# A decoder trunk with experts on one core: the last strip's transposes and the fetched rows' transposes go between the two down pieces of the fifth strip

## The chip, the core and the metric

The kernel runs on one NeuronCore of a Trainium2 chip. TensorE (PE in the profile, its weight loads PEld) multiplies into the PSUM banks; ScalarE (ACT) and VectorE (DVE) work on elements; GpSimd (POOL) and SyncE (SP) here mostly issue transfers. Each engine runs its own queue of instructions in order; queues wait for each other by semaphores. The metric is the device time of one execution, in microseconds.

## What is computed

Two layers of a hybrid decoder over 256 tokens of width 1024, in float32. The second layer's feed-forward part is a mixture of 8 experts, each token going to 2 of them. This is the part that the change touches:

```python
def swiglu(h, w_gate, w_up, w_down):
    return (jax.nn.silu(h @ w_gate) * (h @ w_up)) @ w_down

def moe_ffn(h, w_router, w_gate, w_up, w_down):
    ...
    out = jnp.zeros_like(hf)
    for e in range(N_EXPERTS):
        out = out + gates[:, e:e + 1].astype(hf.dtype) * swiglu(hf, w_gate[e], w_up[e], w_down[e])
```

`w_gate[e]` and `w_up[e]` are 1024 x 2816, `w_down[e]` is 2816 x 1024.

## The kernel before

**Precision.** Each float32 operand is split into a high part (a rounded copy, float32r) and a low part (the rest), and every product is three matmuls: high times high, high times low, low times high (`mm3`, lines 1476 to 1480). Of a weight piece ScalarE makes the high part (`split_expert`, line 696, into `hi_ring`) and VectorE subtracts it from the raw piece (line 1010, into `lo_ring`). Both rings have three slots. The split of piece n + 3 may begin when TensorE has used piece n (`piece_used`), and TensorE begins piece n when `lo_ready` says so.

**Items and pieces.** The loop goes over items: an expert and up to 128 of its tokens, whose rows are gathered. With these inputs 8 items run, one for each expert. An expert's weights come in 33 pieces of 1 MB, in the order of `E_ORDER`. The 2816 hidden columns are cut into six strips (c = 0 to 5), five of 512 and the last of 256. A strip has gate pieces G, up pieces U and down pieces D, two of each (the last strip: one of each). The down pieces of strip c - 1 come behind the gate and up pieces of strip c. So an item ends with G5, U5, D4.0, D4.1, D5 (places 28 to 32 of the order, D4.0 being part 0 of the fifth strip's down pieces), and the next one begins with G0.0, G0.1, U0.0, U0.1. In iteration j of an item, ScalarE and VectorE first split piece j + 2, and then do what else belongs to piece j; the splits of pieces 33 to 35, so counted, belong to the next item.

**From gate and up to down.** With 128 tokens as the output's partitions, gate goes to bank 0 and up to bank 1. ScalarE applies silu (`m_sg`), VectorE multiplies (`m_prod`, line 1431). Then TensorE transposes the product, 128 columns at a time (`transpose_act`, line 1789, into bank 2 or 3), ScalarE copies the high part out (`m_hi`, line 979) and VectorE the low part (`m_lo`, line 1436), and the down pieces multiply these into banks 4 and 5. In general the transposes of strip c are issued behind the gate pieces of strip c + 1. The last strip has none behind it; its transposes stand in front of D5.

**The next item's rows.** GpSimd fetches the next item's rows by an indirect transfer (line 653) once VectorE has written their numbers (line 1454, at U4.0). TensorE transposes them, eight blocks (`fetched_transposes`, line 1774) into banks 6 and 7; ScalarE copies out `sel_hi` (line 953), VectorE `sel_lo` (line 1457). Both are views of hT_hi and hT_lo, and so they are called in the trace; the fetched rows and `m_prod` are views of `xn`. G0.0 waits for `sel_lo`.

**The item's result.** Behind D5 ScalarE copies banks 4 and 5 out as `y_hi` (line 984) and VectorE as `y_lo` (line 1461); the next item scatters them back to token order behind U0.0 and G1.0 (lines 1785 and 1786).

**Order of the queues around the change.** TensorE: D4.0, D4.1, two transposes of strip 5, eight of the fetched rows, D5. ScalarE: split 32, split 33, `m_hi`, split 34, two `sel_hi`, two `y_hi`, split 35. VectorE: split 32, split 33, `m_lo`, split 34, two `sel_lo`, two `y_lo`, split 35. This order is written out by hand. For the last item a branch skips splits 33 to 35.

Of the kernel before, what the change touches and what calls it, by code (L numbers as in the profile page):

```python
# [22 lines left out]
ALU = mybir.AluOpType  # L23
ACT = mybir.ActivationFunctionType
AX = mybir.AxisListType
F32 = mybir.dt.float32
# [5 lines left out]
D = 1024  # L32
# [94 lines left out]
EC = (FF + EW - 1) // EW  # L127
# [74 lines left out]
def build(nc, a, out):  # L202
    with ExitStack() as ctx:
# [8 lines left out]
        bank = [ctx.enter_context(nc.psum_tensor(f"bank{i}", [P, 512], F32)) for i in range(8)]  # L212
# [207 lines left out]
        gathered = sem("gathered")  # L420
# [15 lines left out]
        gathered_lo = sem("gathered_lo")  # L436
# [39 lines left out]
        def last_part(kind, c, part):  # L476
            return part == expert_width(c) // FC - 1
# [7 lines left out]
        def transposed_after(kind, c, part):  # L485

            if kind == "G" and c >= 1 and last_part(kind, c, part):
                return c - 1
            if kind == "D" and c == EC - 2 and last_part(kind, c, part):
                return EC - 1  # L490
            return None

# [188 lines left out]
        def _(act):  # L681
# [268 lines left out]
            def fetched_evac(i):  # L950
                for h in range(2):
                    act.wait_ge(gather_mm, 4 + 2 * i + h + 1)
                    A(sel_hi[:, 4 * h:4 * h + 4, :], bank[6 + h][:].rearrange("p (k s) -> p k s", k=4),
                      ACT.Copy).then_inc(gathered, 1)

            def item(i, more):

                for j, (kind, c, part) in enumerate(E_ORDER):
                    if j + 2 < NFF or more is True:
                        split_expert(i, j + 2)  # L960
                    else:
                        with act.If(more):
                            split_expert(i, j + 2)
                    w = expert_width(c)
                    if kind == "G" and last_part(kind, c, part):
                        act.wait_ge(piece_used, expert_done(i, "G", c))
                        act.wait_ge(prod_done, GU0 + c + i * EC)
                        A(m_sg[:, 0:w], bank[0][:, 0:w], ACT.Silu).then_inc(sg_done, 1)
                    if kind == "U" and c == 2 and part == 0:
                        act.wait_ge(onehot_tmm, i + 1)  # L970
                        A(onehot_t[:], bank[6][:, 0:TT * P].rearrange("p (t s) -> p t s", t=TT),
                          ACT.Copy).then_inc(onehot_tdone, 1)
                    tc = transposed_after(kind, c, part)
                    if tc is not None:
                        act.wait_ge(act_t, tc + 1 + i * EC)
                        if tc >= 2:
                            act.wait_ge(piece_used, expert_done(i, "D", tc - 2))
                        nf = expert_width(tc) // P
                        A(m_hi[:, tc % 2, 0:nf, :], bank[2 + tc % 2][:, 0:nf * P].rearrange("p (f s) -> p f s", f=nf),
                          ACT.Copy).then_inc(act_hi, 1)  # L980
                fetched_evac(i)
                act.wait_ge(piece_used, expert_done(i, "D", EC - 1))
                for h in range(2):
                    A(y_hi[:, h * 512:(h + 1) * 512], bank[4 + h][:], ACT.Copy).then_inc(yhi_done, 1)
# [14 lines left out]
        def _(dve):  # L999
# [418 lines left out]
            def item(i, more, first=False):  # L1418

                for j, (kind, c, part) in enumerate(E_ORDER):  # L1420
                    if j + 2 < NFF or more is True:
                        split_expert(i, j + 2)
                    else:
                        with dve.If(more):
                            split_expert(i, j + 2)
                    w = expert_width(c)
                    if kind == "U" and last_part(kind, c, part):
                        dve.wait_ge(sg_done, GU0 + c + 1 + i * EC)
                        dve.wait_ge(piece_used, expert_done(i, "U", c))
                        dve.wait_ge(act_t, c + i * EC)  # L1430
                        V.tensor_tensor(m_prod[:, 0:w], bank[1][:, 0:w], m_sg[:, 0:w], ALU.mult).then_inc(prod_done, 1)
                    tc = transposed_after(kind, c, part)
                    if tc is not None:
                        nf = expert_width(tc) // P
                        dve.wait_ge(act_hi, GU0 + tc + 1 + i * EC)
                        V.tensor_tensor(m_lo[:, tc % 2, 0:nf, :],  # L1436
                                        bank[2 + tc % 2][:, 0:nf * P].rearrange("p (f s) -> p f s", f=nf),
                                        m_hi[:, tc % 2, 0:nf, :].bitcast(F32), ALU.subtract).then_inc(act_lo, 1)
                    if not first and c <= 1 and kind == ("U", "G")[c] and part == 0:

                        scatter_add(i, 2 * c)
                        scatter_add(i, 2 * c + 1)
                    if kind == "D" and c == 2 and part == 0:

                        dve.wait_ge(onehot_tmm, i + 1)
                        dve.wait_ge(x_upd, XU0 + 4 * i)
                        V.tensor_copy(g_col[:], g_item[:, :, bass.ds(i, 1)].rearrange("p t o -> p (t o)")
                                      ).then_inc(route_v, 1)
                        dve.wait_ge(onehot_done, 3 + 3 * i)
                        make_onehot(i + 1)  # L1450
                        dve.wait_ge(route_v, rv[0] + 1 + i)
                    if kind == "U" and c == 4 and part == 0:
                        dve.wait_ge(slot_mm, i + 1)
                        V.tensor_copy(slot_i[:], bank[7][:, 0:1]).then_inc(slot_ready, 1)  # L1454
                for h in range(2):
                    dve.wait_ge(gathered, 4 + 2 * i + h + 1)
                    V.tensor_tensor(sel_lo[:, 4 * h:4 * h + 4, :], bank[6 + h][:].rearrange("p (k s) -> p k s", k=4),  # L1457
                                    sel_hi[:, 4 * h:4 * h + 4, :].bitcast(F32), ALU.subtract).then_inc(gathered_lo, 1)
                for h in range(2):
                    dve.wait_ge(yhi_done, 2 * i + 1 + h)  # L1460
                    V.tensor_tensor(y_lo[:, h * 512:(h + 1) * 512], bank[4 + h][:],
                                    y_hi[:, h * 512:(h + 1) * 512].bitcast(F32), ALU.subtract).then_inc(ylo_done[h], 1)
# [10 lines left out]
        def _(pe):  # L1473
# [322 lines left out]
            def item(i, first=False):  # L1796
                for j, (kind, c, part) in enumerate(E_ORDER):
# [1 line left out]
                    w = expert_width(c)  # L1799
                    wh, wl = expert_view(hi_of(NA + j), kind, c), expert_view(lo_of(NA + j), kind, c)  # L1800
                    if kind == "D":
                        if c == EC - 1:

                            transpose_act(i, c)
                            pe.wait_ge(onehot_tdone, i + 1)
                            fetched_transposes(i)
                        pe.wait_ge(act_lo, GU0 + c + 1 + i * EC)
                        for f in range(2):
                            for n in range(2):
                                ff = 2 * part + f  # L1810
                                r = mm3(bank[4 + n][:], m_hi[:, c % 2, ff, :], m_lo[:, c % 2, ff, :],
                                        wh[:, f, n * 512:(n + 1) * 512], wl[:, f, n * 512:(n + 1) * 512],
                                        c == 0 and ff == 0, c == EC - 1 and f == 1)
                    else:
                        if part == 0 and c >= 1:
                            if kind == "G":
                                pe.wait_ge(sg_done, GU0 + c + i * EC)
                            else:
                                pe.wait_ge(prod_done, GU0 + c + i * EC)
                        o = bank[0 if kind == "G" else 1][:, 0:w]  # L1820
                        for kk in range(PIECE // w):
                            k = part * (PIECE // w) + kk
                            if kind == "G" and c == 0 and k % 4 == 0:
                                if first:
                                    pe.wait_ge(gathered, 3 + k // 4)
                                else:
                                    pe.wait_ge(gathered_lo, k // 4 - 1 + 2 * i)
                            r = mm3(o, sel_hi[:, k, :], sel_lo[:, k, :], wh[:, kk, :], wl[:, kk, :],
                                    k == 0, k == KT - 1)
# [42 lines left out]
```

## Time and profile before

| | us |
|---|---|
| runs before | 1315.90, 1316.73, 1316.75 |
| median | 1316.73 |
| the profiled execution | 1313.38 |
| its span, from first to last instruction | 1311.6 |
| mean granted clock of TensorE | 0.976 |
| TensorE busy | 1243.0 (95%) |
| VectorE busy | 1021.0 (78%) |
| ScalarE busy | 822.2 (63%) |
| moved by DMA | 349.64 MB, mean 267 GB/s |

The trunk and the first layer fill the first 520 us or so. The rest is the loop over the items, and a short end: adding up and the last norm. Times in the timelines are microseconds from the span's start. A name such as `hT_lo<-bank,hT_hi` says what is written and from what. Matmuls overlap, so the distance from start to start is their true pace, and not their duration.

### The profile page before, as it was taken

How to read it: one execution, taken by the hardware profiler on the slowest of the kernel's cores; microseconds unless marked ns; L12 is line 12 of the kernel's file. 1: busy time of each engine (PE TensorE's matmuls, PEld its weight loads, DVE VectorE, ACT ScalarE, POOL GpSimd, SP SyncE). 2: the span in 40 equal slices, each digit the busy share in tenths (PEclk: the TensorE clock that was granted, in tenths of full speed). 3: DMA queues.
4: the chain of work that ended last, by engine and by line, in shares of the span. 5: the costliest groups of instructions: out<-in, count | busy, mean ns of one | idle time of the engine just before them, and what ended most of it. 6: DMA issues, size and time to landing. Idle time of an engine off the chain costs nothing.

```text
span 1311.6 us, 18352 instructions
## 1 busy us (share of the span) xinstructions
PE 1243.0 (95%) x6658; PEld 1051.2 (80%) x6658; DVE 1021.0 (78%) x1107; ACT 822.2 (63%) x862; POOL 144.9 (11%) x139
## 2 busy tenths in 40 slices
PE   6897999999899888999999999999999999999997
PEld 6866799999787676888888888888888888888885
DVE  5985655445678747888888888988988988988986
ACT  5366544443544745777777777777777776777774
POOL 2860000000068001000000000000000000000000
PEclk9989899999999797999999999999999999999998
DMA  9400665655452039999999999999999999999961
GB/s 332 156 10 1 226 198 192 191 179 181 125 165 76 6 105 393 379 361 354 351 363 355 350 362 355 350 361 355 349 363 356 350 359 361 347 360 362 342 236 48
DMA packets 176165, 349.64 MB, mean 267 GB/s; under 512 B 5719, under 2 KB 63637, under 8 KB 176116
## 3 DMA queue, kind: packets, MB, share of 16 engines
q1 hardware_dynamic: 173852, 341.27, 73.3%
q0 software_dynamic: 2064, 7.17, 1.5%
q8 instruction: 31, 0.51, 0.2%
q10 hardware_dynamic: 200, 0.54, 0.1%
q14 instruction: 18, 0.15, 0.0%
HBM read 346.87 MB, written 2.10 MB: 266 GB/s over the span
## 4 chain that ended last, share of the span: by engine, by line
PE 84%; DVE 8%; ACT 4%; issue 3%; DMA 0%; SPq 0%; POOL 0%; DVEq 0%; ACTq 0%; POOLq 0%
PE bank L1478 26%; PE bank L1480 25%; PE bank L1479 25%; PE bank L1793 1%; DVE cv L1126 1%; ACT hi_ring L696 1%; DVE lo_ring L1005 1%; PE bank L1575 1%; DVE xn L1126 1%; PE bank L1785 1%; ACT hi_ring L690 1%; PE bank L1786 1%; PE bank L1759 1%; PE bank L1615 1%; ACT e_sb L758 1%
## 5 line engine op out<-in xcount | busy, mean ns | idle before, releaser
L1010 DVE TENSOR_TENSOR lo_ring<-raw_m,hi_ring 128x2048 fp32r<-128x2048 f32 x168 | 383.0, 2288 | 54.9 <-ACT hi_ring L696 54.8
L696 ACT ACTIVATE hi_ring<-raw_m 128x2048 fp32r<-128x2048 f32 x168 | 323.0, 1923 | 83.0 <-PE bank L1480 83.0
L1478 PE MATMUL bank<-hi_ring,hT_hi 128*128 128x512 f32 (+2 forms) x896 | 337.7, 377 | 3.4 <-DVE hT_lo L1457 3.4
L1480 PE MATMUL bank<-hi_ring,hT_lo 128*128 128x512 f32 (+2 forms) x896 | 329.7, 368 | 0.0
L1479 PE MATMUL bank<-lo_ring,hT_hi 128*128 128x512 f32 (+2 forms) x896 | 329.4, 368 | 0.0
L1010 DVE TENSOR_TENSOR lo_ring<-raw_a,hi_ring 128x2048 fp32r<-128x2048 f32 x96 | 219.9, 2291 | 41.5 <-ACT hi_ring L696 41.4
L696 ACT ACTIVATE hi_ring<-raw_a 128x2048 fp32r<-128x2048 f32 x96 | 184.2, 1919 | 62.3 <-PE bank L1480 62.3
L1005 DVE TENSOR_TENSOR lo_ring<-raw_a,hi_ring 128x2048 fp32r<-128x2048 f32 (+2 forms) x59 | 132.2, 2246 | 93.9 <-ACT hi_ring L690 93.9
L1478 PEld LDWEIGHTS bank<-hi_ring,hT_hi 128*128 128x128 f32 x896 | 169.9, 190 | 34.8 <-DVE hT_lo L1457 6.4
L1480 PEld LDWEIGHTS bank<-hi_ring,hT_lo 128*128 128x128 f32 x896 | 169.7, 189 | 29.1
L1479 PEld LDWEIGHTS bank<-lo_ring,hT_hi 128*128 128x128 f32 x896 | 170.0, 190 | 27.1 <-issue 0.5
L1478 PE MATMUL bank<-hT_hi,hi_ring 128*128 128x256 f32 (+1 forms) x576 | 165.6, 288 | 1.5 <-DVE hT_lo L1040 1.5
L1479 PE MATMUL bank<-hT_lo,hi_ring 128*128 128x256 f32 (+1 forms) x576 | 164.3, 285 | 0.0
L1480 PE MATMUL bank<-hT_hi,lo_ring 128*128 128x256 f32 (+1 forms) x576 | 164.2, 285 | 0.0
L690 ACT ACTIVATE hi_ring<-raw_a 128x2048 fp32r<-128x2048 f32 (+2 forms) x59 | 109.9, 1862 | 69.1 <-PE bank L1480 62.6
L1478 PE MATMUL bank<-hi_ring,m_hi 128*128 128x512 f32 x352 | 140.2, 398 | 5.5 <-DVE m_lo L1436 5.5
L1479 PE MATMUL bank<-lo_ring,m_hi 128*128 128x512 f32 x352 | 139.4, 396 | 0.0
L1480 PE MATMUL bank<-hi_ring,m_lo 128*128 128x512 f32 x352 | 139.4, 396 | 0.0
L1478 PEld LDWEIGHTS bank<-hT_hi,hi_ring 128*128 128x128 f32 (+1 forms) x576 | 111.5, 194 | 2.7 <-issue 2.1
L1479 PEld LDWEIGHTS bank<-hT_lo,hi_ring 128*128 128x128 f32 (+1 forms) x576 | 111.6, 194 | 0.5
L1480 PEld LDWEIGHTS bank<-hT_hi,lo_ring 128*128 128x128 f32 (+1 forms) x576 | 111.4, 193 | 0.0
L652 POOL TENSOR_TENSOR pool_pad<-half_neg 128x1 f32<-128x1 f32 x8 | 17.3, 2157 | 753.7 <-DVE slot_i L1454 753.7
(277 smaller groups left out, 1399.4 us busy)
## 6 DMA issues: line engine op xcount, KB each, us to landing
raw_m<-in_w_down_exp SPq DMA_DIRECT2D x80, 1024.0 KB, 5.2
raw_a<-in_w_up_exp SPq DMA_DIRECT2D x48, 1024.0 KB, 5.3
raw_m<-in_w_gate_exp SPq DMA_DIRECT2D x48, 1024.0 KB, 5.5
raw_a<-in_w_gate_exp SPq DMA_DIRECT2D x40, 1024.0 KB, 5.5
raw_m<-in_w_up_exp SPq DMA_DIRECT2D x40, 1024.0 KB, 5.9
raw_a<-in_w_in SPq DMA_DIRECT2D x12, 1024.0 KB, 6.6
raw_a<-in_w_gate_dense SPq DMA_DIRECT2D x11, 1024.0 KB, 5.3
raw_a<-in_w_up_dense SPq DMA_DIRECT2D x11, 1024.0 KB, 5.5
```

Of the source, the lines that this page charges most:

```text
L652: nc.gpsimd.tensor_tensor(pool_pad[:], half_neg[:], half_neg[:], ALU.mult).then_inc(pad_done, 1)
L690: A(hi_of(n)[:, 0:w], t[:, 0:w], ACT.Copy).then_inc(hi_ready, 1)
L696: A(hi_of(NA + j), t, ACT.Copy).then_inc(hi_ready, 1)
L758: A(e[:, P:3 * P], s_sb[:, u % 3, P:3 * P], ACT.Exp, scale=-1.0, bias=neg_max[:, u, 1:2], accum_out=row_sum[:, u, 1:2]).then_inc(exp_done, 1)
L1005: V.tensor_tensor(lo_of(n)[:, 0:w], raw_slot(n)[0][:, 0:w], hi_of(n)[:, 0:w].bitcast(F32), ALU.subtract).then_inc(lo_ready, 1)
L1010: V.tensor_tensor(lo_of(NA + j), expert_slot(i, j)[0], hi_of(NA + j).bitcast(F32), ALU.subtract).then_inc(lo_ready, 1)
L1126: conv(V.scalar_tensor_tensor(out, win, wc, old, ALU.mult, ALU.add))
L1478: M(o, lh, rh, start=start, stop=False)
L1479: M(o, lh, rl, start=False, stop=False)
L1480: return M(o, ll, rh, start=False, stop=stop)
L1575: r = M(bank[1 + r3][0:QD, hh * T:(hh + 1) * T], w_uq[:, c, h * QD:(h + 1) * QD], cq[:, c, :], start=c == 0, stop=c == 1)
L1615: r = nc.tensor.transpose(bank[T_BANK[k % 2]][:, b * P:(b + 1) * P], e_sb[:, k % 3, 0, b * P:(b + 1) * P], ident)
```

## The change

TensorE does the transposes of the last strip and of the fetched rows between D4.0 and D4.1, and no longer between D4.1 and D5. ScalarE copies `m_hi` and both `sel_hi` out, and VectorE makes `m_lo` and both `sel_lo`, in the iteration of D4.0: behind split 32 and in front of split 33. Number and size of all instructions stay as they were.

```diff
--- before.py
+++ after.py
@@ -486,7 +486,7 @@
 
             if kind == "G" and c >= 1 and last_part(kind, c, part):
                 return c - 1
-            if kind == "D" and c == EC - 2 and last_part(kind, c, part):
+            if kind == "D" and c == EC - 2 and part == 0:
                 return EC - 1
             return None
 
@@ -978,7 +978,8 @@
                         nf = expert_width(tc) // P
                         A(m_hi[:, tc % 2, 0:nf, :], bank[2 + tc % 2][:, 0:nf * P].rearrange("p (f s) -> p f s", f=nf),
                           ACT.Copy).then_inc(act_hi, 1)
-                fetched_evac(i)
+                    if tc == EC - 1:
+                        fetched_evac(i)
                 act.wait_ge(piece_used, expert_done(i, "D", EC - 1))
                 for h in range(2):
                     A(y_hi[:, h * 512:(h + 1) * 512], bank[4 + h][:], ACT.Copy).then_inc(yhi_done, 1)
@@ -1436,6 +1437,13 @@
                         V.tensor_tensor(m_lo[:, tc % 2, 0:nf, :],
                                         bank[2 + tc % 2][:, 0:nf * P].rearrange("p (f s) -> p f s", f=nf),
                                         m_hi[:, tc % 2, 0:nf, :].bitcast(F32), ALU.subtract).then_inc(act_lo, 1)
+                    if tc == EC - 1:
+                        for h in range(2):
+                            dve.wait_ge(gathered, 4 + 2 * i + h + 1)
+                            V.tensor_tensor(sel_lo[:, 4 * h:4 * h + 4, :],
+                                            bank[6 + h][:].rearrange("p (k s) -> p k s", k=4),
+                                            sel_hi[:, 4 * h:4 * h + 4, :].bitcast(F32), ALU.subtract
+                                            ).then_inc(gathered_lo, 1)
                     if not first and c <= 1 and kind == ("U", "G")[c] and part == 0:
 
                         scatter_add(i, 2 * c)
@@ -1452,10 +1460,6 @@
                     if kind == "U" and c == 4 and part == 0:
                         dve.wait_ge(slot_mm, i + 1)
                         V.tensor_copy(slot_i[:], bank[7][:, 0:1]).then_inc(slot_ready, 1)
-                for h in range(2):
-                    dve.wait_ge(gathered, 4 + 2 * i + h + 1)
-                    V.tensor_tensor(sel_lo[:, 4 * h:4 * h + 4, :], bank[6 + h][:].rearrange("p (k s) -> p k s", k=4),
-                                    sel_hi[:, 4 * h:4 * h + 4, :].bitcast(F32), ALU.subtract).then_inc(gathered_lo, 1)
                 for h in range(2):
                     dve.wait_ge(yhi_done, 2 * i + 1 + h)
                     V.tensor_tensor(y_lo[:, h * 512:(h + 1) * 512], bank[4 + h][:],
@@ -1799,9 +1803,8 @@
                     w = expert_width(c)
                     wh, wl = expert_view(hi_of(NA + j), kind, c), expert_view(lo_of(NA + j), kind, c)
                     if kind == "D":
-                        if c == EC - 1:
-
-                            transpose_act(i, c)
+                        if c == EC - 2 and part == 1:
+                            transpose_act(i, EC - 1)
                             pe.wait_ge(onehot_tdone, i + 1)
                             fetched_transposes(i)
                         pe.wait_ge(act_lo, GU0 + c + 1 + i * EC)
```

## Rows read from the trace of the kernel before

**Rows 1.** Busy time, the loop: PE, PEld, DVE, ACT, POOL, clock, DMA, GB/s.

```profile
527.00:1300.00 773.00, 763.32 (x3623) 630.51 (x3621) 676.62 (x452) 554.34 (x392) 25.53 (x16) 1.00 0.94 342
```

**Rows 2.** Waits: who waited for whom, us in total, times, longest us.

```profile
PEld bank L1478 <- DVE m_lo L1436: 7.4, 8, 1.1
...
PEld bank L1478 <- DVE hT_lo L1457: 6.4, 7, 0.9
...
SPq L566 <- DVE lo_ring L1010: 617.2, 252, 7.9
```

**Rows 3.** Timeline, PE, second item: start us, us, operation, [idle before <-releaser].

```profile
699.22 0.40 PE L1478 MATMUL bank<-hi_ring,m_hi 128*128 128x512 f32 x1
...
702.02 0.38 PE L1793 MATMUL bank<-consts,xn 128*128 128x128 f32 x2
702.24 1.04 PE L1774 MATMUL bank<-consts,xn 128*128 128x128 f32 x8
704.05 0.50 PE L1478 MATMUL bank<-hi_ring,m_hi 128*128 128x512 f32 x1 [0.77 <-DVE m_lo L1436]
704.39 0.40 PE L1479 MATMUL bank<-lo_ring,m_hi 128*128 128x512 f32 x1
```

**Rows 4.** Timeline, DVE, the same place.

```profile
698.37 0.42 DVE L1431 TENSOR_TENSOR xn<-bank,xn 128x256 f32<-128x256 f32 x1
698.71 2.28 DVE L1010 TENSOR_TENSOR lo_ring<-raw_m,hi_ring 128x2048 fp32r<-128x2048 f32 x1
701.37 2.29 DVE L1010 TENSOR_TENSOR lo_ring<-raw_a,hi_ring 128x2048 fp32r<-128x2048 f32 x1 [0.38 <-ACT hi_ring L696]
703.58 0.42 DVE L1436 TENSOR_TENSOR m_lo<-bank,m_hi 128x256 fp32r<-128x256 f32 x1
...
706.87 1.28 DVE L1457 TENSOR_TENSOR hT_lo<-bank,hT_hi 128x512 fp32r<-128x512 f32 x2
...
710.09 2.29 DVE L1010 TENSOR_TENSOR lo_ring<-raw_a,hi_ring 128x2048 fp32r<-128x2048 f32 x1 [0.74 <-ACT hi_ring L696]
```

**Rows 5.** Timeline, ACT, the same place.

```profile
702.44 0.39 ACT L979 ACTIVATE m_hi<-bank 128x256 fp32r<-128x256 f32 x1 [1.11 <-PE bank L1793]
...
704.53 1.07 ACT L953 ACTIVATE hT_hi<-bank 128x512 fp32r<-128x512 f32 x2
707.16 1.09 ACT L984 ACTIVATE hT_hi<-bank 128x512 fp32r<-128x512 f32 x2 [1.56 <-PE bank L1480]
708.14 1.92 ACT L696 ACTIVATE hi_ring<-raw_a 128x2048 fp32r<-128x2048 f32 x1
```

**Rows 6.** Timeline, PE, the last item.

```profile
1295.03 1.04 PE L1774 MATMUL bank<-consts,xn 128*128 128x128 f32 x8
...
1296.46 0.39 PE L1479 MATMUL bank<-lo_ring,m_hi 128*128 128x512 f32 x1
```

**Rows 7.** Timeline, matmuls (PE) and weight loads (PEld), from D5's last matmul.

```profile
706.73 0.40 PE L1480 MATMUL bank<-hi_ring,m_lo 128*128 128x512 f32 x1
...
707.60 0.19 PEld L1478 LDWEIGHTS bank<-hi_ring,hT_hi 128*128 128x128 f32 x1 [0.91 <-DVE hT_lo L1457]
...
707.94 0.39 PE L1479 MATMUL bank<-lo_ring,hT_hi 128*128 128x512 f32 x1
...
713.40 0.39 PE L1479 MATMUL bank<-lo_ring,hT_hi 128*128 128x512 f32 x1
```

**Rows 8.** Timeline, PE: transposes of an earlier strip, with no wait behind them.

```profile
678.70 0.60 PE L1793 MATMUL bank<-consts,xn 128*128 128x128 f32 x4
...
679.37 0.39 PE L1479 MATMUL bank<-lo_ring,hT_hi 128*128 128x512 f32 x1
```

**Rows 9.** The gather: a row of POOL's timeline, and the landing of the eight.

```profile
686.65 1.03 POOL L653 DMA_INDIRECT xn<-rows_dram,slot_i  x1
...
DMA to landing us min/median/max: 4.4/7.0/7.5
```

**Rows 10.** PE's sequencer at the branch: duration ns min/median/max, start us.

```profile
L1848 PEldq COMPARE_BRANCH  x1: 237/237/237, 704.2 to 704.2; - x1
```

## The prediction

> **What bounds the kernel now.** I read busy time by window first. In the loop over experts, 527 to 1300 us, the matmul engine is busy for 763.3 of 773 us, VectorE for 676.6, ScalarE for 554.3 [rows 1]. So TensorE's queue sets the time there, and only its gaps can be gained. Then the list of waits. TensorE's weight loads have two kinds in the loop: 8 waits on `m_lo` (7.4 us) and 7 on `sel_lo`, which the trace calls hT_lo (6.4 us) [rows 2]. That is one pair for each of the 8 items that ran, less one, since no item follows the last. Loads are no bound: SyncE spends 617.2 us in front of the expert loads waiting for VectorE's `lo_ring` to give a raw buffer back [rows 2], so the transfers are ahead of their readers.
>
> Then the order of time at the end of the second item. Splits 33 to 35 are the copies (ScalarE) and subtractions (VectorE) of the next item's first three pieces, G0.0, G0.1 and U0.0. TensorE: D4.1 runs from 699.22, the 2 + 8 transposes follow from 702.02, and D5's first matmul starts only at 704.05 [rows 3]. What it waits for is on VectorE: `m_lo` runs 703.58 to 704.00 [rows 4]. Its input, `m_hi` on ScalarE, started at 702.44 and took 0.39 [rows 5], so it was there at 702.83; VectorE was still in the subtraction of split 33, 701.37 to 703.66 [rows 4]. The wait is thus queueing on VectorE, behind 2.29 us of work that is wanted much later. The second gap is the same trouble once more: `sel_hi` was done at 704.53 + 1.07 = 705.60 [rows 5], but `sel_lo` starts at 706.87 [rows 4], because split 34 stands ahead of it in VectorE's order; its first half is done at 706.87 + 0.64 = 707.5, and G0.0's weights load at 707.60 [rows 7].
>
> **Part 1: what each gap costs.** An undisturbed passage from transposes to matmuls: four transposes are 0.60 us long together from 678.70; the last one starts 0.27 (the length of one) before their end, at 679.03; the second matmul after them starts at 679.37 [rows 8], that is 0.34 later. I count to the second matmul because the first after a wait loads its weights uncovered and pushes the second. Before D5 the last transpose starts at 702.24 + 1.04 - 0.27 = 703.01 and the second matmul at 704.39 [rows 3]: 1.38, so 1.04 lost. In the last item no split 33 stands in the way: last transpose 1295.03 + 1.04 - 0.27 = 1295.80, second matmul 1296.46 [rows 6], 0.66, lost 0.32. The longest of the eight waits is 1.1 us [rows 2], so I take the other six like the second: 7 x 1.04 + 0.32 = 7.6 us. Before G0.0, D5's last matmul starts at 706.73 and the second one of G0.0 at 707.94 [rows 7]: 1.21 against two ordinary steps of 0.23; 0.75 lost, x 7 = 5.25 us. Together 12.9 us is the most that the change can give.
>
> **Part 2: what moves, and what comes out.** The same 10 transposes, 3 evacuations on ScalarE and 3 on VectorE stay; nothing is added or removed. TensorE does the transposes in front of D4.1, so `m_lo` has D4.1 as cover (the 12 matmuls of 699.22 to 702.02, 2.8 us). Worked through for the second item, with the durations of the rows:
> - Transposes from 699.22, if `m_prod` is there: 698.37 + 0.42 = 698.79 [rows 4]. Weights are loaded one step of 0.23 ahead, at 698.99, so 0.2 us in hand. Cost nothing; 0 to 0.1 us per item if that margin is spent.
> - ScalarE: `m_hi` at 699.64 (0.42 after the first transpose, as 702.44 after 702.02 [rows 3, 5]); the two `sel_hi` follow the transposes at 700.07 and 700.55, ScalarE is free at 701.03. Only then comes split 33, and ends at 701.03 + 1.92 = 702.95.
> - VectorE: split 32 to 700.99 as now [rows 4], `m_lo` at once (ready at 701.3), the two `sel_lo` to 702.5, then split 33 from 702.98 to 705.27, where it now begins at 701.37: 1.6 us later.
> - TensorE: ten transposes of 0.109, the last starting at 700.20; second matmul of D4.1 at 700.54, its last at 702.88; D5's last at 705.69. D5 wants `m_lo` at about 702.9 and has it since 701.3: the first gap is gone. G0.0's weights would load at 705.69; `sel_lo` has been there for 3 us, and split 33 comes at 705.27 + 0.05: it clears by 0.37 us. This is the narrowest cover for either gap; beyond it each 0.1 us costs 0.1 us per item.
> - Split 34 waits for D4.1's end, 0.43 after its last matmul starts: 703.31 to 705.23, its subtraction to 707.56; G0.1 wants it at 708.4.
>
> What is late next is U0.0. Split 35 stands behind the two `y_hi` copies, which wait for D5's end. From the start of D5's last matmul (706.73 [rows 7]) to the first `y_hi` (707.16) is 0.43, to split 35 (708.14 [rows 5]) 1.41, to the end of its subtraction (710.09 + 2.29 = 712.38 [rows 4]) 5.65 us. That chain hangs on D5's end and doesn't shrink. G0.0 and G0.1 are 24 matmuls; the 24 steps from 707.94 to 713.40 [rows 7] take 5.46. So with no gap before G0.0 the weight load of U0.0 is due 5.46 after D5's last matmul and gets its piece at 5.65 + 0.05 = 5.70; its second matmul starts at 5.70 + 0.34 = 6.04 instead of 5.46 + 0.46 = 5.92. Today the gap in front of G0.0 hides this. New wait: 0.12 x 7 = 0.8 us. Its bounds: 0 if the copies come a little sooner; 0.45 per item (3 us in all) if VectorE, which must first do split 34 (to 707.56) and two `y_lo` (1.28, as long as the two `sel_lo` [rows 4]), reaches split 35 a third of a microsecond later than the 709.04 that ScalarE sets; by my sum it is free at 708.7.
>
> GpSimd's queue: the fetched rows must be in 2.8 us earlier. The gather's instruction runs from 686.65 to 687.68, and the longest landing of the eight is 7.5 us [rows 9]; even counted from its end that is 695.2, against 699.43 when the first of its transposes is due: 4.2 us in hand, cost nothing. SyncE issues the loads behind splits 33 and 34 up to 1.6 us later; each raw buffer is read again ten pieces of 2.7 us or more later, so this costs nothing. The end of the kernel after the loop keeps its instructions.
>
> **Sum:** 12.9 - 0.8 = 12.1 us. Against the profiled execution (1313.38 us, span 1311.6, so 1.8 around it) that is 1301.3; the median of the runs shown is 1316.73, 3.35 above the profiled one, and the same gain makes 1304.6.
>
> **A rule that speaks against it.** The gap before G0.0 also holds TensorE's jump back to the loop's head. The branch (line 1848) runs at 704.2 and takes 0.24 us [rows 10], when D5's matmuls have just begun; G0.0's weights load at 707.60 [rows 7], 0.1 us after the first half of `sel_lo`. So the jump is hidden and `sel_lo` is the cause. The Trainium skill, "Runtime: NRT & Kernel Launch", section "Instruction fetch mechanics", states that a taken branch whose target lies outside the instruction window forces a fetch before execution can go on; were that the cause, the gap would stay. The trace disagrees at this loop.
>
> **Rivals.**
> 1. The jump sets the second gap, which stays although `sel_lo` is early: 7.6 us gained, 1309.1 us. Against it is the branch 3.4 us before the load [rows 7, 10]; for it, that no row shows G0.0 without a wait. Chance 0.04.
> 2. The second gap reappears in front of G0.0 or U0.0, larger than I have it: split 33 passes its 0.37 us of cover, or VectorE holds split 35. With 0.45 us more per item, 12.1 - 7 x 0.45 = 9.0, 1307.7 us. For it: both covers are below 0.4 us. Against: the waits of the eight items are alike. Chance 0.10.
> 3. Slower: the gather. If the fetched rows land late, TensorE stands in front of D4.1, and ScalarE with it, split 33 behind. It costs nothing up to a landing of 7.5 + 4.2 = 11.7 us, eats the whole gain with 12.1 / 8 = 1.5 us more, and decides for slower by over 0.2% (2.6 us) from 13.5 us on: a landing of 14 us would stall 2.3 x 8 = 18.4 us and give 1304.6 + 18.4 = 1323.0 us, where the rows show 4.4 to 7.5 [rows 9]. Chance 0.03, all of that sign.
> 4. The change doesn't do what it says: ScalarE's two `sel_hi` push split 33, and with it the ring, so far that G0.0 waits for what D5 no longer waits for; 1.7 us later than computed takes the gain, 1316.7 us. Chance 0.03.
>
> **How the numbers follow.** Forecast 0.80: 1304.6 us, its own range 1303 (the new wait is nothing, and the three runs shown differ by 0.85 us) to 1306.5. The range stated, 1302.5 to 1308, also takes in rival 2 and leaves out 1 in 10. A measurement here tells about 0.2% (2.6 us) from no change. Faster by more: forecast, rivals 1 and 2, 0.94; within: 0.03; slower: 0.03.
>
> **What would show it.** In the profile after, TensorE's waits on `m_lo` should be gone in all 8 items, and those on `sel_lo` too; a new wait of TensorE on `lo_ring` of 0.1 to 0.25 us should stand in front of U0.0, 7 times, with the chain of `y_hi` and split 35 in front of it unchanged. Transposes should follow D4.0 without a gap. An item should take about 1.67 us less. I am wrong if TensorE waits in front of the transposes (for `m_prod` or the gather), if G0.0 waits on `lo_ring`, or if its weight load comes late with nothing waited for.

## The result, and the profile after

The changed kernel takes 1304.53 us (median of 6 runs, 1302.71 to 1305.77), the kernel before 1315.48 (6 runs: the three shown ahead and three new ones from 1314.19 to 1315.06). The ratio is 0.9915, 95% interval 0.9902 to 0.9928, so 9.5 to 12.9 us faster. The forecast was 1304.6 us, range 1302.5 to 1308.

| us | before | after |
|---|---|---|
| median | 1315.48 | 1304.53 |
| span of the profiled execution | 1311.6 | 1302.9 |
| first down matmul of the expert loop starts at | 534.3 | 537.7 |
| the loop: from there to the start of its last down matmul | 764.5 | 752.6 |
| one item | 98.80 | 97.14 |

The spans differ by only 8.7 us although the loop gained 11.9. The execution that was profiled after reached the loop 3.4 us later, in code that the change doesn't touch; over the traces of this study the loop begins between 534.3 and 538.4 us, and before's trace is the quickest of them. What goes with it is TensorE's clock: up to the loop its mean granted clock was 0.95 before and 0.94 after, and the same 3062 matmuls there kept TensorE busy for 483.7 us before and 487.6 after. Why the clock differed isn't shown. So I compare loops and items. Where a line is looked at by itself (duration ns min/median/max, first and last start us), the down matmuls of the changed kernel run from 537.7; before they ran 534.3 to 1298.3:

```profile
L1482 PE MATMUL bank<-hi_ring,m_hi x352: 391/397/481, 537.7 to 1289.8; 128*128 128x512 f32 x176
```

An item shows in GpSimd's timeline (start us, us, operation): one gather each, 97.14 us apart.

```profile
688.46 1.03 POOL L653 DMA_INDIRECT xn<-rows_dram,slot_i  x1
...
785.60 1.02 POOL L653 DMA_INDIRECT xn<-rows_dram,slot_i  x1
```

Busy time of the loop by window, with the columns of [rows 1]: the matmul engine is now busy for 763.7 of 764 us.

```profile
527.00:1291.00 764.00, 763.71 (x3638) 633.12 (x3636) 678.90 (x453) 556.15 (x392) 25.53 (x16) 1.00 0.96 348
```

Waits of TensorE's weight loads in the loop (who waited for whom: us in total, times, longest us), beside [rows 2]. The waits on `m_lo` and on `sel_lo` are gone. One kind stands there that was not there before, seven times:

```profile
PEld bank L1482 <- DVE lo_ring L1011: 2.0, 7, 0.3
```

TensorE's timeline at the end of the second item, beside [rows 3]. D4.0 ends, the transposes follow at the ordinary step, and D4.1's second matmul starts 0.34 us after the last transpose:

```profile
700.79 0.39 PE L1484 MATMUL bank<-hi_ring,m_lo 128*128 128x512 f32 x1
701.02 0.38 PE L1797 MATMUL bank<-consts,xn 128*128 128x128 f32 x2
701.24 1.04 PE L1778 MATMUL bank<-consts,xn 128*128 128x128 f32 x8
702.03 0.48 PE L1482 MATMUL bank<-hi_ring,m_hi 128*128 128x512 f32 x1
702.35 0.40 PE L1483 MATMUL bank<-lo_ring,m_hi 128*128 128x512 f32 x1
...
707.50 0.40 PE L1484 MATMUL bank<-hi_ring,m_lo 128*128 128x512 f32 x1
707.73 0.39 PE L1482 MATMUL bank<-hi_ring,hT_hi 128*128 128x512 f32 x1
```

The last two lines are the passage from D5 to G0.0: one step of 0.23 us, where [rows 7] had 0.88. The same place on VectorE, beside [rows 4]: `m_lo` and both `sel_lo` now stand in front of split 33.

```profile
700.52 2.28 DVE L1011 TENSOR_TENSOR lo_ring<-raw_m,hi_ring 128x2048 fp32r<-128x2048 f32 x1
702.72 0.42 DVE L1437 TENSOR_TENSOR m_lo<-bank,m_hi 128x256 fp32r<-128x256 f32 x1
703.05 1.28 DVE L1443 TENSOR_TENSOR hT_lo<-bank,hT_hi 128x512 fp32r<-128x512 f32 x2
704.80 4.56 DVE L1011 TENSOR_TENSOR lo_ring<-raw_a,hi_ring 128x2048 fp32r<-128x2048 f32 x2 [0.47 <-ACT hi_ring L696]
709.28 1.28 DVE L1465 TENSOR_TENSOR hT_lo<-bank,hT_hi 128x512 fp32r<-128x512 f32 x2
710.85 4.49 DVE L1011 TENSOR_TENSOR lo_ring<-raw_a,hi_ring 128x2048 fp32r<-128x2048 f32 x2 [0.29 <-ACT hi_ring L696]
```

ScalarE, beside [rows 5]:

```profile
701.44 0.38 ACT L979 ACTIVATE m_hi<-bank 128x256 fp32r<-128x256 f32 x1 [1.09 <-PE bank L1797]
701.88 1.09 ACT L953 ACTIVATE hT_hi<-bank 128x512 fp32r<-128x512 f32 x2
702.85 1.92 ACT L696 ACTIVATE hi_ring<-raw_a 128x2048 fp32r<-128x2048 f32 x1
...
707.93 1.09 ACT L985 ACTIVATE hT_hi<-bank 128x512 fp32r<-128x512 f32 x2 [0.90 <-PE bank L1484]
```

And the weight load that now waits, U0.0's:

```profile
713.20 0.19 PEld L1482 LDWEIGHTS bank<-hi_ring,hT_hi 128*128 128x128 f32 x1 [0.28 <-DVE lo_ring L1011]
```

### The profile page after: what moved, and what is told of

Same layout as the page of the kernel before. It is cut to its first block, busy times and chain, and to the rows that moved or that the text cites. A ratio compares the mean times of both kernels' runs of the same rounds, so it can differ in the third digit from the quotient of the medians.

```text
span 1302.9 us, 18352 instructions
## 1 busy us (share of the span) xinstructions
PE 1243.3 (95%) x6658; PEld 1052.8 (81%) x6658; DVE 1020.0 (78%) x1107; ACT 822.2 (63%) x862; POOL 144.8 (11%) x139
## 4 chain that ended last, share of the span: by engine, by line
PE 87%; DVE 7%; ACT 3%; issue 2%; DMA 0%; SPq 0%; POOL 0%; POOLq 0%; DVEq 0%; ACTq 0%
PE bank L1482 26%; PE bank L1484 26%; PE bank L1483 26%; PE bank L1797 1%; DVE cv L1127 1%; PE bank L1579 1%; DVE lo_ring L1006 1%; DVE xn L1127 1%; PE bank L1619 1%; ACT hi_ring L690 1%; PE bank L1789 1%; PE bank L1763 1%; PE bank L1778 1%; PE bank L1561 1%; PE bank L1790 1%
```

## Experiments

The theory: both gaps are queueing in VectorE's in-order queue behind subtractions that are wanted later, and both the order of the queues and the place of the transposes are needed to remove them. Rivals: each gap is its own, and each half of the move brings its own share; the longer cover on TensorE suffices; the order on VectorE and ScalarE suffices. "Loop" is the time from the first to the last down matmul's start in the profiled execution (before 764.5, after 752.6); ratios are to the kernel before, measured on the same chip. The runs stand on three chips (e1 to e4, e5 to e7, e8 and e9), so that across them ratios and loops can be compared, and medians only roughly. "The clock falls" below means that the granted clock of TensorE drops from 2.4 to 1.2 GHz for 3.4 us; the last section has the rows.

| | median, us | ratio, 95% interval | loop, us |
|---|---|---|---|
| e1, strip's transposes only | 1312.31 | 0.9985 (0.9969 to 1.0002) | 762.3 |
| e2, fetched rows' transposes only | 1324.41 | 1.0078 (1.0050 to 1.0105) | 773.6 |
| e3, VectorE's order kept | 1326.93 | 1.0087 (1.0055 to 1.0119) | 776.1 |
| e4, changed kernel again | 1304.64 | 0.9917 (0.9885 to 0.9950) | 752.6 |
| e5, only the order of VectorE and ScalarE | 1325.08 | 1.0068 (1.0051 to 1.0085) | 774.0 |
| e6, gather three pieces later | 1327.57 | 1.0086 (1.0069 to 1.0103) | 778.2 |
| e7, 0.9 us more on ScalarE | 1307.00 | 0.9926 (0.9908 to 0.9944) | 756.0 |
| e8, y copies behind split 35 | 1302.68 | 0.9900 (0.9884 to 0.9915) | 751.3 |
| e9, changed kernel, beside e8 | 1302.94 | 0.9907 (0.9891 to 0.9923) | 752.7 |

**e1: only the strip's transposes move.** Against the kernel before:

```diff
-            if kind == "D" and c == EC - 2 and last_part(kind, c, part):
+            if kind == "D" and c == EC - 2 and part == 0:
...
+                        if c == EC - 2 and part == 1:
+                            transpose_act(i, EC - 1)
                         if c == EC - 1:
-
-                            transpose_act(i, c)
                             pe.wait_ge(onehot_tdone, i + 1)
```

> Half of the change: the strip's two transposes, m_hi and m_lo go between D4.0 and D4.1; the fetched rows' eight transposes, sel_hi and sel_lo stay where they were. Queueing theory (both gaps are VectorE's in-order queue): the gap before D5 goes (8 items), but the one before G0.0 grows from 0.75 to about 1.5 us, because sel_lo still stands behind split 34 and TensorE now gets there sooner. Sum: 7 x 0.3 + 0.3 = 2.4 us faster than before, about 1313. Rival (only the strip's transposes matter, each gap is its own): 7.6 us faster than before, the second gap stays at 0.75.

The loop got 2.2 us shorter, 2.4 were expected; the ratio by itself doesn't reach beyond its noise. TensorE's waits in the loop show where the rest went: none on `m_lo` any more, but those on `sel_lo` grew from 6.4 us [rows 2] to nearly double.

```profile
PEld bank L1478 <- DVE hT_lo L1457: 11.9, 7, 1.8
```

VectorE and TensorE at the second item's end show why: D5 runs earlier, and `sel_lo` (707.87) is still behind split 34.

```profile
705.66 2.29 DVE L1010 TENSOR_TENSOR lo_ring<-raw_a,hi_ring 128x2048 fp32r<-128x2048 f32 x1 [0.21 <-ACT hi_ring L696]
...
706.96 0.40 PE L1480 MATMUL bank<-hi_ring,m_lo 128*128 128x512 f32 x1
...
707.87 1.28 DVE L1457 TENSOR_TENSOR hT_lo<-bank,hT_hi 128x512 fp32r<-128x512 f32 x2
...
708.95 0.39 PE L1479 MATMUL bank<-lo_ring,hT_hi 128*128 128x512 f32 x1
```

From D5's last matmul to G0.0's second one it is 1.99 us, less 0.46 for two steps: 1.53 lost, where 1.5 was expected and 0.75 was lost before. A gap that is closed in front of a second one moves into it.

**e2: only the fetched rows' transposes move.** Against the changed kernel (not shown here: `fetched_evac` on ScalarE and the two `sel_lo` on VectorE get the condition `kind == "D" and c == EC - 2 and part == 0`, so that they keep the iteration of D4.0):

```diff
-            if kind == "D" and c == EC - 2 and part == 0:
+            if kind == "D" and c == EC - 2 and last_part(kind, c, part):
                 return EC - 1
...
-                        if c == EC - 2 and part == 1:
+                        if c == EC - 1:
                             transpose_act(i, EC - 1)
+                        if c == EC - 2 and part == 1:
                             pe.wait_ge(onehot_tdone, i + 1)
```

> The other half: the fetched rows' eight transposes, sel_hi and sel_lo go between D4.0 and D4.1; the strip's two transposes, m_hi and m_lo stay in front of D5. Queueing theory: the gap before G0.0 goes, the one before D5 grows from 1.04 to about 2.4 us (m_lo stands behind split 33, which the two sel_hi copies push 1.4 us later, and the eight transposes no longer cover it); per item 0.8 us more than before with the new wait of 0.12 before U0.0, sum about 6 us slower than before. Rival (each gap is its own): 5.2 us faster than before.

The gap before G0.0 went, and the one before D5 became 2.4 us, as expected:

```profile
PEld bank L1482 <- DVE m_lo L1437: 18.1, 8, 2.4
```

The loop got 9.1 us longer than before, not 6. The items account for it: five of seven take 99.57 us, 0.77 more than before, which makes 5.4 with all seven; the last item loses 0.9 more; and two items take 100.97, 1.4 us above the others. In both of these the clock falls behind the gap. So the mechanism was as expected, and this price was missing.

**e3: VectorE keeps its order.** TensorE and ScalarE as in the changed kernel; on VectorE only:

```diff
                     tc = transposed_after(kind, c, part)
+                    if kind == "D" and c == EC - 2:
+                        tc = EC - 1 if last_part(kind, c, part) else None
```

> TensorE and ScalarE as in the changed kernel, but VectorE keeps the old order: split 33 first, then m_lo and the two sel_lo in the iteration of D4.1. Queueing theory: m_lo comes only after split 33, which ScalarE's three copies have pushed to 705.3 in the prediction's clock; D5 waits about 2.5 us, the gap before G0.0 is gone, and the kernel is 5 to 7 us slower than before. Rival (the longer cover on TensorE is what brings the gain, whatever VectorE's order): as fast as the changed kernel, some 11 us faster than before.

The second item on VectorE: `m_lo` is again behind split 33, and split 33 itself later.

```profile
706.23 2.29 DVE L1011 TENSOR_TENSOR lo_ring<-raw_a,hi_ring 128x2048 fp32r<-128x2048 f32 x1 [2.00 <-ACT hi_ring L696]
708.44 0.42 DVE L1439 TENSOR_TENSOR m_lo<-bank,m_hi 128x256 fp32r<-128x256 f32 x1
```

In the third item D5's first matmul waits 2.49 us for it:

```profile
808.87 0.47 PE L1484 MATMUL bank<-hi_ring,m_hi 128*128 128x512 f32 x1 [2.49 <-DVE m_lo L1439]
```

The loop is 11.6 us longer than before: 1.05 in each of seven items (7.4), less 0.3 in the last, and 1.5 more in three items with the fallen clock. Without the clock's part that is 7.1, just past the 5 to 7 expected. The cover on TensorE alone brings nothing; the rival that it suffices is out.

**e5: only the order on VectorE and ScalarE.** The changed kernel with TensorE's transposes back in front of D5:

```diff
                     if kind == "D":
-                        if c == EC - 2 and part == 1:
+                        if c == EC - 1:
                             transpose_act(i, EC - 1)
```

> ScalarE's and VectorE's order as in the changed kernel (m_hi, both sel_hi, m_lo, both sel_lo in front of split 33), but TensorE's transposes stay in front of D5. Queueing theory: D5 finds m_lo early, its gap is about 0.3 us as in the last item of the kernel before; but split 33 now waits for all three copies, ends some 2.4 us after D5's end, and G0.0 waits for lo_ring instead of sel_lo. Per item 2.6 us of gaps against 1.8, so about 6 us slower than before, more if the long gap lowers the granted clock in some items. Rival (the order of the queues is enough, the transposes' place does not matter): as fast as the changed kernel, some 11 us faster than before.

TensorE's waits in the loop: `m_lo` is down to 0.3 us each, which shows directly that the first gap was queueing on VectorE, and G0.0 waits 2.3 us in front of its weights. The list puts these loads down to "issue"; the matmuls behind them have the name.

```profile
PEld bank L1482 <- issue: 15.8, 7, 2.3
PE bank L1482 <- DVE lo_ring L1011: 12.8, 7, 1.8
PEld bank L1482 <- DVE m_lo L1437: 2.4, 8, 0.3
```

The loop is 9.5 us longer than before: four items of 99.48, three of 101.05 with the fallen clock (0.68 x 7 + 1.57 x 3 = 9.5). Without the clock's part it is 4.8, where about 6 was expected. The order of the queues alone loses as well.

**e4 and e9: the changed kernel again.**

> The changed kernel once more beside the others on the same chip, to see how much of a difference between two executions comes from the trunk ahead of the loop. An item takes 97.14 us in its trace and 98.80 in that of the kernel before; if the gain is all in the loop, the item's time repeats to 0.02 us and the ratio is 0.990 to 0.993, while the time of the trunk moves by some us from execution to execution.

> The changed kernel beside the one with the y copies moved: 1304.5, an item 97.14 us, the gap of 0.28 us in front of U0.0 in 7 items.

Both loops took 752.6 and 752.7 us, the items 97.13 to 97.16 after the first, and the ratios are 0.9917 and 0.9907. The loop began at 538.4 and 535.7 us: most of the spread between executions lies ahead of it.

**e6: how much time the gather has.** The changed kernel with

```diff
-                    if kind == "U" and c == 4 and part == 0:
+                    if kind == "D" and c == 3 and part == 1:
                         dve.wait_ge(slot_mm, i + 1)
...
-                    if kind == "G" and c == 4 and part == 0:
+                    if kind == "U" and c == 4 and part == 1:
                         slots_of(i)
```

> The changed kernel with the slot numbers taken three pieces (8.2 us) later, so that the gather starts at about 9.0 us before the first transpose is due instead of 12.8 minus nothing: issue 4.6 us before the transposes. With a landing of 4.4 to 7.5 us the fetched rows come up to 2.9 us too late. If the prediction's margin (4 to 5 us in hand) is right, three pieces are more than it: TensorE waits 0 to 3 us per item for the transfer in front of the transposes, ScalarE and split 33 behind it, and the kernel is 5 to 25 us slower than the changed one. If the rows are really there much sooner than the landing figure says, nothing changes: 1304.5.

TensorE now waits for the transfer in front of the fetched rows' transposes:

```profile
PE bank L1778 <- DMA xn<-rows_dram,slot_i: 17.8, 7, 3.2
```

Seven items wait, 2.2 to 3.4 us each, and in four of them the clock falls; the loop is 25.6 us longer than the changed kernel's. The median is 1327.57 us; the execution that was profiled was the longest of the four, 1330.98. This is rival 3 of the prediction made to happen. The expectation had the gather's start 4.6 us before the transposes. In the second item it is at 698.91, 6.9 us before they were due (705.77). But its instruction took 2.8 us instead of 1.0, and the landings were 6.1 to 10.0 us (median 9.2), longer than the 4.4 to 7.5 that it reckoned with. Why they were longer isn't shown. In the changed kernel itself the longest landing is 8.3 us (line of the gather, min/median/max):

```profile
DMA to landing us min/median/max: 4.5/7.7/8.3
```

With the second item's gather at 688.46 that is 696.8, and its transposes start at 701.24: 4.5 us in hand, counted from the gather's start. The prediction's 4.2 was counted from its instruction's end, 1.03 us later; from the start it would have been 5.3.

**e7: how wide the cover of G0.0 is.** The changed kernel with one more ScalarE copy between `sel_hi` and split 33:

```diff
                         fetched_evac(i)
+                        if not first:
+                            act.wait_ge(extra_done, i)
+                        A(ht_lo[:, 0, :], ht_lo[:, 1, :].bitcast(F32), ACT.Copy).then_inc(extra_done, 1)
...
```

> The changed kernel with one more ScalarE copy of 128 x 1024 (about 0.92 us) between sel_hi and split 33, into a tile that nobody reads. In the changed kernel's trace split 33's subtraction ends 0.38 us before G0.0's weights are due. Theory (that is the cover, beyond it every 0.1 us costs 0.1): G0.0 waits about 0.54 us for lo_ring, 0.1 more for the uncovered load, and the 0.12 us in front of U0.0 goes: 0.5 x 7 = 3.7 us slower than the changed kernel, an item takes 97.65 us. Rival (the ring has slack elsewhere that takes up a microsecond): no change, 97.14.

The loop is 3.4 us longer than the changed kernel's (3.7 expected), an item takes 97.62 us. G0.0's load waits, for split 33, and, against what I expected, U0.0's does still:

```profile
708.27 0.19 PEld L1486 LDWEIGHTS bank<-hi_ring,hT_hi 128*128 128x128 f32 x1 [0.71 <-issue]
...
713.79 0.19 PEld L1486 LDWEIGHTS bank<-hi_ring,hT_hi 128*128 128x128 f32 x1 [0.22 <-DVE lo_ring L1015]
```

On VectorE split 33 runs from 705.85, and the two `y_lo` from 710.26 with split 35's subtraction right behind them from 711.46, with no idle time between; ScalarE had its part of split 35 done at 710.93. So here it is VectorE that is late for U0.0, not ScalarE.

```profile
705.85 4.49 DVE L1015 TENSOR_TENSOR lo_ring<-raw_a,hi_ring 128x2048 fp32r<-128x2048 f32 x2 [1.42 <-ACT hi_ring L697]
710.26 1.28 DVE L1469 TENSOR_TENSOR hT_lo<-bank,hT_hi 128x512 fp32r<-128x512 f32 x2
711.46 4.48 DVE L1015 TENSOR_TENSOR lo_ring<-raw_a,hi_ring 128x2048 fp32r<-128x2048 f32 x2
```

**e8: the y copies behind split 35.** The changed kernel, with the copies of an item's result taken in the next item's first iteration (and once after the loop):

```diff
                             split_expert(i, j + 2)
+                    if j == 0 and not first:
+                        y_evac(i)
...
+            y_evac(n_items)
```

and the same on VectorE with `y_low`.

> The changed kernel with the two y_hi copies behind split 35 on ScalarE and y_lo behind split 35 on VectorE (in the next item's first iteration), since the scatter wants them only after U0.0. Theory (the 0.28 us gap in front of U0.0 is the chain D5's end, y_hi, split 35): split 35 starts 0.97 us sooner, the gap goes, its price of 0.12 us comes back: an item takes 97.02 us instead of 97.14, 0.8 us in all, 1303.8; less than the run-to-run spread, so the item time in the trace decides. Rival (the gap in front of U0.0 has another cause, as the sequencer's handling of the wait): it stays at 97.14.

ScalarE's split 35 (here at 706.57) now stands in front of `y_hi`:

```profile
706.57 1.92 ACT L696 ACTIVATE hi_ring<-raw_a 128x2048 fp32r<-128x2048 f32 x1 [0.89 <-PE bank L1496]
708.39 1.06 ACT L989 ACTIVATE hT_hi<-bank 128x512 fp32r<-128x512 f32 x2
```

No wait of TensorE's weight loads is left in the loop, so the chain of `y_hi` and split 35 was the cause. An item takes 96.96 us, 0.18 less than 97.14 where 0.12 was expected; the loop is 1.4 us shorter than in e9, which ran beside it. In whole runs that is too little to tell (1302.68 against 1302.94), so this kernel beats the changed one only by its trace; against the kernel before its ratio is 0.9900 (0.9884 to 0.9915).

## Why the prediction was right

**The bound and the causes.** "TensorE's queue sets the time, only its gaps can be gained" held: an item got shorter by 1.66 us, where 1.67 was forecast. That both gaps are queueing on VectorE is shown by e1 to e5: one part of the change by itself gave 2.2 us (e1) or lost 9 to 12 (e2, e3, e5). VectorE's order and the transposes' place on TensorE are both needed.

**Part 1, 12.9 us at most.** No wait on `m_lo` or `sel_lo` is left. With the new wait's price as measured in e8 (0.18 x 7 = 1.3) the loop's 11.9 us make 13.2 for the two gaps, where 12.9 was worked out: e8, which has neither gap nor the new wait, gives 1.84 per item (98.80 to 96.96), where 1.04 + 0.75 was worked out.

**Part 2, the order of time.** The prediction gave it in before's clock, D4.0 ending where the first transpose starts, at 699.22; after, that is 701.02, so 1.80 is added:

| | foretold + 1.80 | after |
|---|---|---|
| `m_lo` starts | 702.71 | 702.72 |
| first `sel_hi` | 701.87 | 701.88 |
| split 33 on VectorE | 704.78 | 704.80 |
| D5's last matmul | 707.49 | 707.50 |
| first `y_hi` | 707.92 | 707.93 |
| split 35 on VectorE | 710.84 | 710.85 |
| U0.0's weights load | 713.19 | 713.20 |

(`m_lo` starts 0.08 before split 32 ends, as everywhere in VectorE's rows.) The cover of `m_prod` in front of the transposes was enough: no gap there. The cover in front of G0.0 held too, but the 0.37 us was somewhat too large. In e7 split 33 came 0.95 us later against D5's last matmul, and G0.0's load came 0.67 after that matmul, so 0.28 had covered. The difference lies in the step from the subtraction's end to the load, 0.13 us at this place in e7 and e5, where the prediction put 0.05.

**The new wait.** Seven waits in front of U0.0, of 0.28 to 0.30 us of idle weight loading each, stand where 0.1 to 0.25 was foretold. The term that was mis-sized is its price: 0.12 us, worked out up to the second matmul behind the wait; taking it away gave 0.18 (e8). Laid beside e8 from D5's last matmul on, the second matmul of U0.0 is 0.13 us late, and ten steps further on it is 0.18, which stays. This is 0.06 per item, 0.4 us in all.

**The sum.** 12.1 us forecast, 11.9 in the loop, 9.5 to 12.9 in whole runs. Two small misses of opposite sign stand in it: the gaps were worth 0.3 us more than the 12.9, and the new wait cost 0.4 to 0.5 more than the 0.8. Laid onto the median that was shown (1316.73) it gave 1304.6, against 1304.53 measured. That the last digit fits is luck: three more runs of before were quicker and brought its median to 1315.48.

**The rivals.** The jump: G0.0's first matmul follows D5's last by 0.23 us across the loop's branch, so nothing of the second gap was the jump's. The rule of the Trainium skill ("Runtime: NRT & Kernel Launch", "Instruction fetch mechanics") speaks of a target outside the instruction window. In the trace after, the last instruction transfer of the loop starts at 705 us and the next one at 1259, so from the third item on none was fetched for the jump; the prediction's "disagrees" says too much, since the rule's condition was then not met, as far as the transfers show. The larger gap in front of U0.0 (rival 2) didn't come, but e7 shows how near it is: 0.9 us more on ScalarE make VectorE late there. The gather (rival 3) has 4.5 us in hand; e6 went past it and lost 25.6 us. The prediction had worked out 18.4 for 2.3 us in each of 8 items; the seven waits of the weight loads in e6 add up to 19.4, and the four falls of the clock make up the rest. Rival 4, split 33 pushed so far by the two `sel_hi` that G0.0 waits, didn't come: ScalarE took it up at 702.85, by the prediction's clock 702.83. e5 shows what it looks like: there the transposes come late, and G0.0 waits 2.3 us for split 33.

## What to carry to other kernels

When a tuned matmul engine waits, look at what stands in front of the awaited instruction in the in-order queue of the engine that makes it: often it is not the work but its place. Changing that place and moving the source early enough to feed it are one change; done in part, it gave 2 us here or lost 9 to 12. Then follow the chain that hangs on the new, earlier end of the step: here the next wait, 0.28 us in front of U0.0, had been hidden by the old gap, and it could be worked out from the rows of before.

## What was not expected

A long gap on TensorE can cost more than its length. Gaps are counted here as idle time of the weight loads. In e2, e3, e5 and e6, whose longest gaps in the loop are 2.4, 2.9, 2.3 and 3.4 us, the granted clock fell from 2.4 to 1.2 GHz for 3.4 us in two, three, three and four of the items. Each fall began 0.1 to 1.5 us after the gap's end, though in the 90 us ahead of the gap TensorE had shown none over 0.35 us. Busy time by window in e3 around such a place (columns as in [rows 1]):

```profile
805.00:809.80 4.80, 2.31 (x10) 1.58 (x9) 3.71 (x4) 2.97 (x2) 0.00 (x0) 1.00 0.98 362
809.80:813.20 3.40, 3.40 (x9) 2.65 (x9) 2.31 (x2) 0.00 (x0) 0.00 (x0) 0.50 0.89 299
813.20:820.00 6.80, 6.80 (x30) 5.42 (x30) 4.89 (x4) 5.67 (x6) 0.00 (x0) 1.00 0.57 166
```

The gap ends at 808.87, and behind 809.8 the matmuls go at a step of 0.43 us instead of 0.23:

```profile
811.22 0.63 PE L1485 MATMUL bank<-lo_ring,m_hi 128*128 128x512 f32 x1
811.65 0.63 PE L1486 MATMUL bank<-hi_ring,m_lo 128*128 128x512 f32 x1
```

Each fall cost 1.4 to 1.6 us in the item's time. Gaps of up to 1.8 us (e1) or 1.1 (before) never brought it in the loop. Why only some of the equal gaps did stays open, and so does the shortest gap that can.
